# A later table of positions for the attention steps of two mixers, and the weight splits after them

## The reference

```python
q, k, v = jnp.split(proj, 3, axis=-1)      # rope on q and k
p = masked_softmax(s, key_pos <= tq)        # two maps for each of 8 heads
a = p[:, :, 0] - lam_val * p[:, :, 1]
o = rms_norm(einsum(a, v), subln_g) * (1.0 - lambda_init);  return o @ w_out
```

```python
logit_own = einsum(q, k) * scale + bias_own   # masked above the diagonal
return softmax(logit_own) @ v_own @ w_o
```

## Time and profile before

| | us |
|---|---|
| median of 3 runs | 1328.12 |
| lowest and highest | 1325.83 and 1328.39 |
| the profiled execution | 1326.24 |
| its span | 1324.4 |
| PE busy | 1219.8 (92%) |
| DVE busy | 847.3 (64%) |
| ACT busy | 574.4 (43%) |
| mean granted TensorE clock | 0.939 |

### The profile page before, as it was taken

How to read it: one execution, slowest core, us unless ns; L and a number is a source line. 1 busy time by engine, 2 the same in 40 slices (tenths; PEclk the granted TensorE clock), 3 DMA queues, 4 the chain that set the end, 5 groups by cost and what they waited for, 6 DMA issues and landing times.

```text
span 1324.4 us, 18386 instructions
## 1 busy us (share of the span) xinstructions
PE 1219.8 (92%) x7598; PEld 1071.9 (81%) x7598; DVE 847.3 (64%) x1276; ACT 574.4 (43%) x837; POOL 44.6 (3%) x86
## 2 busy tenths in 40 slices
PE   4989998999999988789999957999999899899997
PEld 3984776899998867579999847999988697899996
DVE  5662544587777766668777765977776445655554
ACT  5302231554444544455444455444446443744442
POOL 1010000000000000000000000000001100000000
PEclk9998556999999998899999978999999999899999
DMA  7933010488776423238877603977755432265530
GB/s 286 205 122 128 35 63 30 150 306 323 281 278 223 187 96 128 96 122 321 332 278 278 217 28 157 363 282 280 283 190 193 141 141 99 99 236 186 185 139 32
DMA packets 35746, 248.96 MB, mean 188 GB/s; under 512 B 4272, under 2 KB 4288, under 8 KB 6608
## 3 DMA queue, kind: packets, MB, share of 16 engines
q1 hardware_dynamic: 26352, 189.13, 38.3%
q0 software_dynamic: 9168, 57.56, 12.7%
q10 hardware_dynamic: 144, 1.11, 0.2%
HBM read 243.06 MB, written 4.19 MB: 187 GB/s over the span
## 4 chain that ended last, share of the span: by engine, by line
PE 81%; DVE 11%; ACT 4%; issue 2%; DMA 1%; DVEq 0%; SPq 0%; ACTq 0%
PE bank L1143 68%; DVE wlo L598 3%; PE bank L1318 2%; ACT whi L366 1%; PE bank L1502 1%; PE bank L1332 1%; DMA raw<-in_stream 1%; PE bank L1374 1%; DVE x L616 1%; DVE work L614 1%; PE bank L1221 1%; DVE ul L643 1%; PE bank L1385 1%; PE bank L1339 1%; PE bank L1341 1%
## 5 line engine op out<-in xcount | busy, mean ns | idle before, releaser
L598 DVE TENSOR_TENSOR wlo<-raw,whi 128x2048 fp32r<-128x2048 f32 x175 | 398.7, 2283 | 133.1 <-ACT whi L366 133.0
L1143 PE MATMUL bank<-uh,whi 128*128 128x256 f32 x1280 | 370.6, 289 | 2.9 <-DVE ul L643 2.9
L1143 PE MATMUL bank<-ul,whi 128*128 128x256 f32 x1280 | 363.6, 284 | 0.0
L1143 PE MATMUL bank<-uh,wlo 128*128 128x256 f32 x1280 | 363.5, 284 | 0.0
L366 ACT ACTIVATE whi<-raw 128x2048 fp32r<-128x2048 f32 x175 | 332.4, 1906 | 71.3 <-PE bank L1143 62.3
L1143 PEld LDWEIGHTS bank<-uh,whi 128*128 128x128 f32 x1280 | 246.9, 193 | 11.0 <-issue 8.9
L1143 PEld LDWEIGHTS bank<-ul,whi 128*128 128x128 f32 x1280 | 247.0, 193 | 4.7 <-issue 2.6
L1143 PEld LDWEIGHTS bank<-uh,wlo 128*128 128x128 f32 x1280 | 246.8, 193 | 0.0
L1143 PE MATMUL bank<-whi,hh 128*128 128x512 f32 x544 | 214.9, 395 | 0.0
L1143 PE MATMUL bank<-wlo,hh 128*128 128x512 f32 x544 | 212.9, 391 | 0.0
L1143 PE MATMUL bank<-whi,hl 128*128 128x512 f32 x544 | 212.2, 390 | 0.0
(11 more groups left out here) (229 smaller groups left out, 1157.8 us busy)
## 6 DMA issues: line engine op xcount, KB each, us to landing
raw<-in_stream SPq DMA_DIRECT2D x178, 1024.0 KB, 4.9
qk<-in_w_mod POOLq DMA_DIRECT2D x48, 1024.0 KB, 6.0
bias_rows<-PT POOLq DMA_DIRECT2D x1, 3072.0 KB, 36.3
u<-bias_rows POOLq DMA_DIRECT2D x16, 128.0 KB, 2.5
con<-in_con ACTq DMA_DIRECT2D x1, 1083.5 KB, 6.9
x<-in_x SPq DMA_DIRECT2D x2, 512.0 KB, 8.3
vo<-in_fin_g POOLq DMA_DIRECT2D x2, 512.0 KB, 4.3
out_y<-vo SPq DMA_DIRECT2D x2, 512.0 KB, 2.6
```

The lines of the kernel that those rows point to most:

```text
L598: nc.vector.tensor_tensor(wlo[:, c % RING, 0:w], raw[:, raw_index(c) % RING, 0:w], whi[:, c % RING, 0:w].bitcast(fp32), ALU.subtract).then ...
L1143: ins = mm(out, st, mv, start=start and i == 0, stop=stop and i == 2, skip_group_check=True)
```

## The change

1. Each phase has tables of its own. `combine` gets a table too, `JOIN_AT`. Most S keep their place in "d" or move by a quarter, and T and V move later by up to four quarters. In "b" S moves earlier, and T and V too.
2. On ACT `hi_upto` moves from q 0, ahead of the attention steps, to q 1, after them.
3. Chunks 6 and 7 run one after the other (`rows_of_values`): chunk 6 over all tokens, then chunk 7. Each is counted as `used` at its end.
4. The copies of the second 512 columns of the values wait for chunk 7 as a whole. In both versions ACT does them in stretch 8, q 0.
5. In "d" the copy to `PT` moves from DVE to ACT, ahead of ACT's other work of that quarter.

```diff
+SCORE_AT = {"d": {(4, 3): 0, (5, 2): 1, (6, 3): 2, (7, 2): 3, (10, 3): 4, (11, 1): 5, (12, 3): 6, (13, 1): 7},
+            "b": {(4, 1): 0, (4, 3): 1, (6, 1): 2, (6, 3): 3, (10, 1): 4, (10, 3): 5, (12, 1): 6, (12, 3): 7}}
+JOIN_AT = {(5, 3): 0, (6, 2): 1, (7, 3): 2, (8, 2): 3, (11, 2): 4, (12, 0): 5, (13, 2): 6, (14, 0): 7}
+TURN_AT = {"d": {(6, 1): (0, 0), (7, 0): (1, 0), (8, 1): (2, 0), (9, 0): (3, 0),
+                 (11, 3): (4, 0), (12, 1): (5, 0), (13, 3): (6, 0), (14, 1): (7, 0)},
+           "b": {(5, 1): (0, 0), (5, 2): (0, 1), (5, 3): (1, 0), (6, 0): (1, 1), (7, 1): (2, 0), (7, 2): (2, 1),
+                 (7, 3): (3, 0), (8, 0): (3, 1), (11, 1): (4, 0), (11, 2): (4, 1), (11, 3): (5, 0), (12, 0): (5, 1),
+                 (13, 1): (6, 0), (13, 2): (6, 1), (13, 3): (7, 0), (14, 0): (7, 1)}}
+VALUE_AT = {"d": {(6, 3): 0, (7, 2): 1, (9, 0): 2, (9, 2): 3, (12, 0): 4, (12, 2): 5, (14, 0): 6, (14, 2): 7},
+            "b": {(5, 3): 0, (6, 1): 1, (7, 3): 2, (8, 1): 3, (11, 3): 4, (12, 1): 5, (13, 3): 6, (14, 1): 7}}
+OUT_AT = {"d": {(8, 1): 0, (10, 1): 1, (13, 2): 2, (14, 3): 3},
+          "b": {(6, 3): 0, (8, 3): 1, (12, 3): 2, (14, 3): 3}}
...
             for i, q in QUARTERS:
-                if q == 0:
-                    if i and i <= 12 and MIXER[i - 1][0] == "v" and MIXER[i - 1][2] == 1:
-                        value_copies(MIXER[i - 1][1], 0, DIFF + i - 1, d_v)
-                    hi_upto(min(DIFF + i + 3, MLP1 + 1))
-                if (i, q) in SCORE_AT:
-                    pair_exps("d", SCORE_AT[i, q])
...
+                if q == 0 and 1 <= i <= 12 and MIXER[i - 1][0] == "v" and MIXER[i - 1][2] == 1:
+                    value_copies(MIXER[i - 1][1], 0, DIFF + i - 1, d_v)
+                if (i, q) in TURN_AT["d"]:
+                    p = TURN_AT["d"][i, q][0]
+                    act.wait_ge(s_tr["d"], p + 1)
+                    if p >= 1:
+                        act.wait_ge(s_pv["d"], p)
+                    nc.scalar.activation(PT[:, 0, :], bank[5][:, 0:384], ACT.Copy).then_inc(s_pt["d"], 1)
+                if (i, q) in SCORE_AT["d"]:
+                    pair_exps("d", SCORE_AT["d"][i, q])
...
+                if (i, q) in OUT_AT["d"]:
+                    pair_upper(1, OUT_AT["d"][i, q], lam[:, 6:7])
+                if q == 1:
+                    hi_upto(min(DIFF + i + 3, MLP1 + 1))
...
-                if q == 0:
+                if (i, q) in SCORE_AT["b"]:
+                    pair_exps("b", SCORE_AT["b"][i, q])
+                if (i, q) in OUT_AT["b"]:
+                    pair_upper(2, OUT_AT["b"][i, q], one)
+                if q == 1:
                     hi_upto(min(MOBA + i + 3, MLP3 + 1))
...
-                if (i, q) in TURN_AT and TURN_AT[i, q][1] == 0:
-                    turned_copy("d", *TURN_AT[i, q])
-                if (i, q) in SCORE_AT:
-                    pair_maxima("d", SCORE_AT[i, q])
-                if (i, q) in VALUE_AT and VALUE_AT[i, q] % 2:
-                    sub_norm(VALUE_AT[i, q] // 2)
...
+                if (i, q) in SCORE_AT["d"]:
+                    pair_maxima("d", SCORE_AT["d"][i, q])
+                if (i, q) in JOIN_AT:
+                    combine(JOIN_AT[i, q])
+                if (i, q) in VALUE_AT["d"] and VALUE_AT["d"][i, q] % 2:
+                    sub_norm(VALUE_AT["d"][i, q] // 2)
+                if (i, q) in OUT_AT["d"]:
+                    pair_lower(1, OUT_AT["d"][i, q], lam[:, 6:7])
                 if q == 1:
                     lo_upto(min(DIFF + i + 3, MLP1 + 1))
-                if (i, q - 2) in SCORE_AT or (i - 1, q + 2) in SCORE_AT:
-                    combine(SCORE_AT.get((i, q - 2), SCORE_AT.get((i - 1, q + 2))))
...
+            def rows_of_values(m, g, steps):
+
+                pe.wait_ge(lo_ready, m + 1)
+                for t in range(NT):
+                    ins = half_values(m, g, t, None, lambda t, q: steps(2 * t + q % 2))
+                ins.then_inc(used, 1)
...
-                elif kind == "v" and k == 0:
-                    pe.wait_ge(d_add, 3)
-                    both_halves(DIFF + i, None, lambda t, q, i=i: (beside("d", 1, i + t)(q), dswap(i + t, q)))
+                elif kind == "v" and j == 1:
+                    if k == 0:
+                        pe.wait_ge(d_add, 3)
+                    rows_of_values(DIFF + i, k, steps)
```

More of the change, by code:

```diff
@@ L498, in value_copies @@
                 for t in range(NT):
-                    if t == 0:
-                        act.wait_ge(v_ps, base + h + 1)
+                    if t == 0 and h == 0:
+                        act.wait_ge(v_ps, base + 1)
                     else:
@@ L565, in _ @@
                     elif k == 1:
-                        value_copies(j, 2, MOBA + i - 1, b_v)
+                        value_copies(j, 1, MOBA + i - 1, b_v)
                         if i == 2:
                             spread_copy(3, cb, 6)
-                if q == 0:
+                if (i, q) in SCORE_AT["b"]:
[3 more added lines that the diff above has]
+                if q == 1:
                     hi_upto(min(MOBA + i + 3, MLP3 + 1))
-                if (i, q) in SCORE_AT:
-                    pair_exps("b", SCORE_AT[i, q])
-                if (i, q) in OUT_AT:
-                    pair_upper(2, OUT_AT[i, q], one)
             act.wait_ge(mod_ready, 3)
@@ L735, in turned_copy @@
             def turned_copy(ph, p, c):
[L736 removed]
+                n = 2 * p + c
                 dve.wait_ge(s_tr[ph], n + 1)
@@ L1103, in _ @@
             for i, q in QUARTERS:
[L1104 to L1109, removed]
+                if (i, q) in TURN_AT["b"]:
+                    turned_copy("b", *TURN_AT["b"][i, q])
+                if (i, q) in SCORE_AT["b"]:
+                    pair_maxima("b", SCORE_AT["b"][i, q])
+                if (i, q) in VALUE_AT["b"] and VALUE_AT["b"][i, q] % 2:
+                    j = VALUE_AT["b"][i, q] // 2
                     dve.wait_ge(s_exp["b"], 4 * j + 4)
@@ L1118, in _ @@
                     ins.then_inc(o_sc, 1)
-                if (i, q) in OUT_AT:
-                    pair_lower(2, OUT_AT[i, q], one)
+                if (i, q) in OUT_AT["b"]:
+                    pair_lower(2, OUT_AT["b"][i, q], one)
                 if q == 1:
@@ L1416, in steps @@
                 def steps(q):
[L1417 to L1424, removed]
+                    if (i, q) in VALUE_AT[ph]:
+                        pair_values(ph, r, VALUE_AT[ph][i, q])
+                    if (i, q) in TURN_AT[ph]:
+                        pair_turn(ph, *TURN_AT[ph][i, q])
+                    if (i, q) in SCORE_AT[ph]:
+                        pair_scores(ph, SCORE_AT[ph][i, q])
+                    if (i, q) in OUT_AT[ph]:
+                        pair_out(r, OUT_AT[ph][i, q])
                 return steps
@@ L1573, in _, with both_halves @@
                     ins.then_inc(oc_ps, 1)
-            def both_halves(m, e=None, steps=None):
+            def rows_of_values(m, g, steps):
[3 more added lines that the diff above has]
+                ins.then_inc(used, 1)
+            def both_halves(m, e):
                 for g in range(2):
@@ L1579, in both_halves @@
                     for g in range(2):
-                        ins = half_values(m + g, g, t, None if e is None else ul_no(e, t), steps)
+                        ins = half_values(m + g, g, t, ul_no(e, t))
                         if t == 1:
@@ L1584, in both_halves @@
                             ins.then_inc(v_ps, 1)
-                        if e is not None and t == 0 and g == 0:
+                        if t == 0 and g == 0:
                             norm(e, 1)
@@ L1645, in _ @@
                     spread_col(mod[:, 64:72], 6)
-                elif kind == "v" and k == 0:
-                    pe.wait_ge(b_copied, 3)
-                    both_halves(MOBA + i, None, lambda t, q, i=i: beside("b", 2, i + t)(q))
+                elif kind == "v" and j == 1:
+                    if k == 0:
+                        pe.wait_ge(b_copied, 3)
+                    rows_of_values(MOBA + i, k, beside("b", 2, i))
                 elif kind == "f":
```

15 lines of the change are left out of this document (2 added, 13 removed).

## The result

The changed kernel takes 1346.41 us (median, 1344.95 to 1347.05), the kernel before 1328.2 in the same job. The ratio is 1.014, 95% interval 1.0122 to 1.0157: slower, by 18.2 us. The prediction had the sign and 1337.6 us, and its range ended at 1345.0, so the time lies outside it. The profiled execution took 1347.05 us, 20.8 more than the one of before. That difference is what the traces can be asked for.

What follows compares the result with a forecast made beforehand. PE, busy 92% of the span, was taken as the bound, leaving only waits and clock to change. Waits +7.5, clock +4.8 and -0.9 absorbed make +11.4 on 1326.24, so 1337.6 us; range 1321 to 1345.

Steps and rivals of the forecast that it cites:

- What bounds the kernel: PE is busy 92% of the span; only idle time and clock in the two mixers, about 36 us, can be won.
- what made the long waits: Chunk 6 counted late holds ACT's split and O's upper part, making the 7.84 and 5.58 us waits; edits 2 and 3 clear this.
- The walk: New tables put on the old time axis, engine by engine: waits 21.8 us in "d", 15.0 in "b", together 7.5 more.
- T6 and T4: The T steps of pairs 6 and 4 in "d": waits of 4.2 and 4.15 us, released just behind a split on DVE.
- Low clock: PE's slow stretches after waits: seven at 1.6 us, 11.2 against 6.4 before, so 4.8 us more.
- S4: Scores of pair 4 in "d", at (10, 3): a wait of 1.4 us behind rope sum 5, with no low stretch counted.
- (12, 2): Quarter in "d" where PE waits for the last rope sum: 2.9 us, low stretch counted at one in three.
- both pairs in "b": Neighbouring waits at T21 and V2, and again six stretches later: 2.15 and 1.5 us, one low stretch in three each.
- What T3 absorbs: The wait for pair 3's T in "d" runs on DVE's time and takes in about 0.9 us of lost clock.
- slower still: Rival: every wait of 1.5 us and more ends in a low stretch at 2.06 us, giving 1345.8 us; chance 0.13.
- The long waits did go and the rest wasn't covered: Judges the rival that ACT's steps overlap better, long waits go and new ones stay small: 1309 us, chance 0.14.
- The clock didn't stay up: Judges the rival that waits come as walked but too short to lower the clock: +1.1 us, 1327; chance 0.14.

Runs made afterwards that it cites:

- Filling the waits: Changed kernel with matmuls that compute nothing put on PE in eleven of its waits and the one before the last rope sum, about half as many as first tried: 1330.98 us.
- the run with the long waits filled: Changed kernel with matmuls that compute nothing put on PE at its seven long waits alone, the short ones left empty: 1335.05 us.
- splits first: Changed kernel with ACT's splits back at quarter 0, ahead of the attention steps, in both phases: 1309.67 us, ratio 0.9868 to the kernel before.

## Why the prediction was right or wrong

**What bounds the kernel, and what made the long waits.** Right. PE's idle time and clock in the two mixers were nearly all that moved; 1.0 us came between them. Chunk 6 counted late was what held 7.84 and 5.58: with that edit alone they are 5.14 and 2.07.

**The walk.** Right, and closer than its prices deserve: 7.5 us more of waits forecast, 7.7 measured, and no single wait off by more than 0.6 us. That the sums agree so well is partly luck, as the single errors go both ways. T6 and T4, given as the test, wait 4.45 and 4.55 behind a split, and the first V in "b" 3.78 (3.7 forecast). That the order on ACT is the cause is shown by undoing it (36.7 us) and by doing it alone (30.4 us the other way).

**Low clock.** This is the step that failed. It priced a low stretch at 1.6 us, and counted one for each wait over 3.3 us and one in three for the shorter ones: seven, 11.2 us, 4.8 more than before, 3.9 with what was to be absorbed. The trace has ten, three of them twice as long, 19.9 us, 12.3 more than before. The price itself held for a single stretch: the seven of 3.4 us cost some 1.6 us each, half of what lies outside the waits. The count and the length were wrong. S4 (1.79 us), (12, 2) and both pairs in "b" brought one each, where a rate of one in three, taken from three old waits near 2.1 us, had allowed one for (12, 2) and the pairs together and none for S4. And those behind T6, O3 and V6 were 6.8 us long and cost some 2.8 us each. Long stretches were there to be seen: 0.60 over 11 us is 8.8 us at half clock. But of the old stretches of 10.2 and 6.8 us, 5.8 and 2.8 us lay in the waits of 7.84 and 5.58 us, where they cost nothing, so they looked like single ones. Behind the changed kernel's waits, none over 4.55 us, nearly all of the low stretches lies in work, 40 of 44 us. (The four old ones cost 7.6 us, where the sum had 6.4.) What T3 absorbs is 0.65 us (it waits 0.39, and 1.04 where the clock stayed up), not 0.9. Filling the waits shows the term by itself: 15.4 us of time, 17.6 with the longer waits, where the sum had 11.2.

**The sum and the range.** The rival "slower still" said that every wait of 1.5 us and more ends in a low stretch, and put that at 1345.8, with nine stretches and 12.1 us more of clock. That is close to what happened, ten and 12.3, and I gave it 0.13. Its rule isn't shown by it: in the run with the long waits filled, the same pairs in "b" brought none. I also cut the range at 1345.0, just short of that rival's own time. My range should have gone to the bound worked out for the unknown term.

**The other rivals.** The long waits did go and the rest wasn't covered. The clock didn't stay up. Edit 5 was priced between 0.8 us less and 1.4 more. The copy takes 0.49 us on ACT, as taken (0.56 on DVE). With splits first the edit saves 1.6 us of waits, and perhaps 3 in all, which I had not seen: DVE no longer waits for T ahead of its split, and the wait at (12, 2) goes from 1.22 to 0.

**What the change is made of.** Tables -8, chunk-wise values -4, the two together -15, the copies up to -3 more (not clear of noise): edits worth 18 us together. Splits behind the attention steps cost 37 on top of them. Only that was visible in the total.

## What to carry to other kernels

Where two engines pass work on in program order, a step isn't late because it waits for its own input but because of what stands ahead of it in the list: T4 waits 4.55 us with ACT's split behind the exponentials and 1.28 with it ahead. Moving a helper step "behind the urgent ones" on one engine puts it ahead of the urgent ones on the next, if that engine waits for it. Walk the lists engine by engine before moving anything.
